# The first two modulation sections by column blocks, and the first three output chunks k-pair by k-pair

## The reference, cut to what matters

```python
c_act = silu(c)                                   # (1, 2048)
for layer in range(2):
    mod = c_act @ ada_w[layer] + ada_b[layer]     # (2048 x 12288) weights
    shift_t, scale_t, gate_t, shift_m, scale_m, gate_m = split(mod, 6)
    h = rms_norm(x, norm_g[layer, 0]) * (1 + scale_t) + shift_t
    y = mixer(h, ...)                             # layer 0: qkv = h @ w_qkv
    x = x + gate_t * y
    h = rms_norm(x, norm_g[layer, 1]) * (1 + scale_m) + shift_m
    x = x + gate_m * square(relu(h @ w1)) @ w2
```

## Time and profile before

| | us |
|---|---|
| median of three runs (2586.28 to 2590.52) | 2586.66 |
| the profiled execution: its own time | 2587.83 |
| its span, first to last instruction | 2586.0 |
| TensorE busy | 2403.0 (93%) |
| VectorE busy | 1848.6 (71%) |
| ScalarE busy | 1185.4 (46%) |
| bytes moved | 665.23 MB, 257 GB/s over the span |

### The profile page before, as it was taken

How to read it: one execution, slowest core, us unless ns; L and a number is a source line. 1 busy time by engine, 2 the same in 40 slices (tenths; PEclk the granted TensorE clock), 3 DMA queues, 4 the chain that set the end, 5 groups by cost and what they waited for, 6 DMA issues and landing times.

```text
span 2586.0 us, 27843 instructions
## 1 busy us (share of the span) xinstructions
PE 2403.0 (93%) x10901; PEld 1970.1 (76%) x10901; DVE 1848.6 (71%) x2145; ACT 1185.4 (46%) x1931; POOL 72.9 (3%) x128
## 2 busy tenths in 40 slices
PE   0299999997999999999998989999899999999999
PEld 0288888876787888888887877777687888888887
DVE  7778786877788677677776767877796555555554
ACT  1256556564543443443445664554543443443442
POOL 1100000000100000000001010000100000000000
PEclk9599999999999999999999999999999999999999
DMA  8688696866788777777785867856696555555554
GB/s 358 270 296 306 220 342 233 328 252 236 292 302 308 261 282 275 276 289 267 280 301 207 316 230 282 312 210 254 263 368 211 189 187 187 187 186 188 187 187 163
DMA packets 150466, 665.23 MB, mean 257 GB/s; under 512 B 16864, under 2 KB 17344, under 8 KB 120896
## 3 DMA queue, kind: packets, MB, share of 16 engines
q1 hardware_dynamic: 150336, 663.46, 70.3%
HBM read 661.30 MB, written 2.10 MB: 257 GB/s over the span
## 4 chain that ended last, share of the span: by engine, by line
PE 75%; DVE 12%; ACT 5%; DMA 4%; issue 4%; POOL 0%; SPq 0%; DVEq 0%; ACTq 0%
PE main L359 24%; PE main L361 24%; PE main L360 24%; DVE acc L916 5%; DVE w_lo L899 3%; DMA w_raw<-w 2%; PE tr L372 2%; ACT w_hi L644 1%; DMA ada_raw<-ada 1%; ACT st_a L684 1%; PE tr L414 1%; DMA qT<-ada 1%; ACT sm L717 1%; PE tr L435 0%; ACT st_b L670 0%
## 5 line engine op out<-in xcount | busy, mean ns | idle before, releaser
L644 ACT ACTIVATE w_hi<-w_raw 128x1024 fp32r<-128x1024 f32 x800 | 844.1, 1060 | 1105.0 <-DMA w_raw<-w 1104.6
L899 DVE TENSOR_TENSOR w_lo<-w_raw,w_hi 128x1024 fp32r<-128x1024 f32 x800 | 971.6, 1222 | 438.4 <-ACT w_hi L644 434.9
L359 PE MATMUL main<-w_hi,hT_hi 128*128 128x512 f32 x2176 | 869.4, 400 | 7.0 <-DVE w_lo L899 2.9
L361 PE MATMUL main<-w_hi,hT_lo 128*128 128x512 f32 x2176 | 851.5, 391 | 0.0
L360 PE MATMUL main<-w_lo,hT_hi 128*128 128x512 f32 x2176 | 850.8, 391 | 0.0
L916 DVE SCALAR_TENSOR_TENSOR acc<-ada_raw,c_act,acc 128x2048 f32<-128x2048 f32 x194 | 455.7, 2349 | 50.2 <-DMA ada_raw<-ada 47.8
L359 PEld LDWEIGHTS main<-w_hi,hT_hi 128*128 128x128 f32 x2176 | 411.6, 189 | 93.4 <-DVE w_lo L899 5.2
L361 PEld LDWEIGHTS main<-w_hi,hT_lo 128*128 128x128 f32 x2176 | 410.5, 189 | 86.9
L360 PEld LDWEIGHTS main<-w_lo,hT_hi 128*128 128x128 f32 x2176 | 411.3, 189 | 83.4 <-issue 1.2
L359 PE MATMUL main<-w_hi,mid_hi 128*128 128x512 f32 x1024 | 406.1, 397 | 0.0
L361 PE MATMUL main<-w_hi,mid_lo 128*128 128x512 f32 x1024 | 404.0, 395 | 0.0
(11 more groups left out here) (155 smaller groups left out, 1166.7 us busy)
## 6 DMA issues: line engine op xcount, KB each, us to landing
w_raw<-w SPq DMA_DIRECT2D x800, 512.0 KB, 3.4
ada_raw<-ada SPq DMA_DIRECT2D x208, 1024.0 KB, 6.5
qT<-ada SPq DMA_DIRECT2D x16, 1024.0 KB, 7.2
gate<-bias_rows SPq DMA_DIRECT2D x4, 1024.0 KB, 6.5
xs<-x SPq DMA_DIRECT2D x1, 2048.0 KB, 9.2
out<-xs SPq DMA_DIRECT2D x4, 512.0 KB, 5.3
st_a<-lamb SPq DMA_DIRECT2D x1, 256.0 KB, 4.7
gain_rot_sb<-gain_rot SPq DMA_DIRECT2D x1, 160.0 KB, 2.9
```

The source lines that it names most:

```text
L359: pe.matmul(acc_ps[:, :], hi[:, kt, tc], w_hi[:, s, wc], start=(kt == 0), stop=False)
L361: last = pe.matmul(acc_ps[:, :], lo[:, kt, tc], w_hi[:, s, wc], start=False, stop=(kt == PK * pairs - 1))
L644: act.activation(w_hi[:, s, :], w_raw[:, s, :], ACT.Copy).then_inc(hi_done, 1)
L899: dve.tensor_tensor(w_lo[:, s, :], w_raw[:, s, :], w_hi[:, s, :].bitcast(F32), ALU.subtract).then_inc(lo_done, 1)
```

## The change

- The host lays out the first two sections of `ada` by column blocks. Round j (0 to 7) has four pieces of 1 MB, a = 0 to 3. Piece a holds four k-tiles, and of each the 256 shift and 256 scale columns that belong to pair j of k-tiles of `h`.
- Of a piece's four k-tiles VectorE adds three (two of the last piece) into 512 columns of `acc`, each step waiting for the one before; TensorE does the rest as f32 products with one moving column, four for each k-tile (`first_columns`), and sums `acc` over partitions with a column of ones (`first_total`). Both accumulate in one bank, `tr[1]`. VectorE then makes the 2 + 2 columns of factor and shift for pair j (`first_modulation`).
- The first three chunks (q, k, v of quad 0) arrive interleaved: for each pair of k-tiles a piece of q, of k and of v, between pieces a=1 and a=2 of the round. TensorE multiplies pair j-1 in round j (`first_piece`) into six banks: `main[1]`, `main[0]`, and `sc` with `ov`.
- x is loaded second; the gains come after the 32 pieces; ScalarE squares x before the angles. The zero attention step is dropped.
- After the first stage q and k of quad 0 are read out of `main`, and v out of `sc`, `ov`, during chunk 3. The 48 later `ada` pieces of this stage go to the 15 chunks left: 2, 3, 4, 4 in group 0; 3, 3, 4, 3, 3, 3 in group 1; 3, 3, 4, 3, 3 in group 2. Two sections are then in work at once; the second is summed in `gate`.

```diff
@@ host layout
+    first = [np.concatenate([w[:, cols(j, PK * P)] for w in ada[0:2]], axis=1) for j in range(PIECES)]
+    ada[0:2] = [w.reshape(FIRST_PIECES, KT // FIRST_PIECES, P, NC).transpose(0, 2, 1, 3).reshape(-1, D) for w in first]
+    stream[0:3] = [np.stack([w.reshape(PIECES, P, PK * NC) for w in stream[0:3]], axis=1).reshape(-1, PK * NC)]
@@ constants
-ADA_QKV = after((0, 5, 7), (0, 5, 7), (0, 2, 4, 6), (0, 5, 7), (0, 5, 7))
+FIRST_PIECES = 4
+PE_TILES = (1, 1, 1, 2)
+ADA_QKV = [((g, c), j) for g, c, js in (
+    (0, 2, (0, 7)), (0, 3, (0, 5, 7)), (0, 4, (0, 2, 5, 7)), (0, 5, (0, 1, 2, 7)), (1, 0, (0, 5, 7)),
+    (1, 1, (0, 5, 7)), (1, 2, (0, 2, 4, 6)), (1, 3, (0, 5, 7)), (1, 4, (0, 5, 7)), (1, 5, (0, 2, 7)),
+    (2, 0, (0, 5, 7)), (2, 1, (0, 5, 7)), (2, 2, (0, 2, 4, 6)), (2, 3, (0, 5, 7)), (2, 4, (0, 5, 7))) for j in js]
@@ sync
+            def first_ada(i):
+                s = i % len(ada_start)
+                if i >= len(ada_start):
+                    sp.wait_ge(ada_used, ADA_SLOTS + i + 1 - len(ada_start))
+                    sp.wait_ge(ada_mm, i + 1 - len(ada_start))
+                sp.dma_start(ada_start[s], av[i]).then_inc(ada_start_in[s], 16)
+            for j in range(PIECES):
+                for a in range(FIRST_PIECES):
+                    if a == 2:
+                        for _ in range(3):
+                            weight_piece()
+                    first_ada(FIRST_PIECES * j + a)
...
+            sp.wait_ge(ada_mm, 2 * KT)
@@ tensor
+            def first_columns(j, a):
+                i = FIRST_PIECES * j + a
+                fills, s = divmod(i, len(ada_start))
+                pe.wait_ge(ada_start_in[s], 16 * (fills + 1))
+                last = None
+                for k in range(FIRST_PIECES - PE_TILES[a], FIRST_PIECES):
+                    kt = FIRST_PIECES * a + k
+                    for c in range(4):
+                        last = pe.matmul(tr[1][:, 4 * j + c:4 * j + c + 1],
+                                         ada_start[s][:, k * NC + c * P:k * NC + (c + 1) * P],
+                                         c_act[:, kt:kt + 1], start=(a == 0 and last is None), stop=False)
+                last.then_inc(ada_mm, 1)
+            def first_total(j):
+                pe.wait_ge(ada_used, ADA_SLOTS + FIRST_PIECES * (j + 1))
+                for c in range(4):
+                    at = (j % 2) * NC + c * P
+                    last = pe.matmul(tr[1][:, 4 * j + c:4 * j + c + 1], acc[:, at:at + P], ones[:, 0:1],
+                                     start=False, stop=(c == 3))
+                last.then_inc(col_full, 1)
+            def first_piece(j, part):
...
+                if part == 0:
+                    pe.wait_ge(hT_split, n["split"].up())
+                pe.wait_ge(lo_done, n["w"].n)
+                banks = (main[1], main[0], (sc, ov))[part]
+                for kt in range(PK * j, PK * (j + 1)):
...
+            for j in range(PIECES):
+                if j:
+                    pe.wait_ge(mod_done, j)
+                first_columns(j, 0)
+                first_columns(j, 1)
+                if j:
+                    first_piece(j - 1, 0)
+                first_transposes(j)
+                if j:
+                    first_piece(j - 1, 1)
+                    first_piece(j - 1, 2)
+                first_columns(j, 2)
+                first_columns(j, 3)
+                first_total(j)
+            for part in range(3):
+                first_piece(PIECES - 1, part)
@@ scalar
+            for j in range(PIECES):
+                for _ in range(3):
+                    split()
+                high(j, (S_SCALE_T0, S_SHIFT_T0), True)()
+            act.wait_ge(gain_in, 16 * 3)
...
+                    chunk(PIECES, {3: [qk_stats(1, 5), qk_scale(1)], 5: [move_tile0(q4, g), qk_stats(0, 6)],
+                                   6: [qk_scale(0)], 7: [first_values], 8: [move_tile0(k4, GROUPS + g)]})
@@ vector
+            for j in range(PIECES):
+                first_ada(j, 0)
+                if j == 0:
+                    sum_x()
+                else:
+                    pair(j - 1, True)()
+                first_ada(j, 1)
+                if j == 0:
+                    x_recip()
+                for _ in range(3):
+                    split()
+                first_ada(j, 2)
...
+                first_ada(j, 3)
+                first_modulation(j)
```

More of the change, by code:

```diff
@@ L297, in _ @@
+            sp.dma_start(subg[:, :], subg_in.partition_broadcast(P)).then_inc(gain_in, 16)
+            sp.wait_ge(ada_mm, 2 * KT)
+            for g in range(GROUPS):
+                for c in range(0 if g else 2, 6 if g < GROUPS - 1 else 5):
+                    if (g, c) == (GROUPS - 1, 2):
+                        sp.wait_ge(scale_added, 1)
+                        bias(0, 0)
+                    chunk((g, c), ada=ADA_QKV)
             for ch in range(4):
@@ new lines, in first_piece @@
+            def first_piece(j, part):
+                if j == 0 and part < 2:
+                    claim_main(1 - part)
+                if j == 0 and part == 2:
+                    pe.wait_ge(x_sq, 4)
+                if part == 0:
+                    pe.wait_ge(hT_split, n["split"].up())
+                n["w"].up()
+                s = (n["w"].n - 1) % SLOTS
+                pe.wait_ge(lo_done, n["w"].n)
+                banks = (main[1], main[0], (sc, ov))[part]
+                for kt in range(PK * j, PK * (j + 1)):
+                    wc = cols(kt % PK, NC)
+                    for t in range(T):
+                        tc = cols(t, P)
+                        pe.matmul(banks[t][:, :], hT_hi[:, kt, tc], w_hi[:, s, wc], start=(kt == 0), stop=False)
+                        pe.matmul(banks[t][:, :], hT_hi[:, kt, tc], w_lo[:, s, wc], start=False, stop=False)
+                        last = pe.matmul(banks[t][:, :], hT_lo[:, kt, tc], w_hi[:, s, wc], start=False,
+                                         stop=(kt == KT - 1))
+                last.then_inc(mm_done, 1)
@@ L788, in _ @@
             act.activation(c_act[:, :], vec[:, V_C, :], ACT.Exp, scale=-1.0).then_inc(c_exp, 1)
+            act.wait_ge(x_in_done, 16)
+            for c in range(4):
+                squares(c)
+            root()
             act.wait_ge(lam_dot, 1)
@@ L915, in accumulate, with first_ada @@
                     dve.wait_ge(ada_used, a - 1 + ADA_SLOTS)
-                    ins = dve.scalar_tensor_tensor(out=acc[:, :], in0=piece, scalar=c_act[:, kt:kt + 1],
-                                                   in1=acc[:, :], op0=ALU.mult, op1=ALU.add)
+                    ins = dve.scalar_tensor_tensor(out=total[:, :], in0=piece, scalar=c_act[:, kt:kt + 1],
+                                                   in1=total[:, :], op0=ALU.mult, op1=ALU.add)
                 ins.then_inc(ada_used, 1)
-            def chunk(ch, pieces, side=None, ada=(), kt0=0):
+            def first_ada(j, a):
+                i = FIRST_PIECES * j + a
+                fills, s = divmod(i, len(ada_start))
+                dve.wait_ge(ada_start_in[s], 16 * (fills + 1))
+                total = acc[:, cols(j % 2, NC)]
+                tiles = FIRST_PIECES - PE_TILES[a]
+                for k in range(tiles):
+                    piece, c = ada_start[s][:, cols(k, NC)], c_act[:, FIRST_PIECES * a + k:FIRST_PIECES * a + k + 1]
+                    if a == 0 and k == 0:
+                        ins = dve.tensor_scalar(total, piece, c, None, ALU.mult)
+                    else:
+                        if k == 0:
+                            dve.wait_ge(ada_used, ADA_SLOTS + i)
+                        ins = dve.scalar_tensor_tensor(out=total, in0=piece, scalar=c, in1=total,
+                                                       op0=ALU.mult, op1=ALU.add)
+                    if k < tiles - 1:
+                        chained(ins)
+                ins.then_inc(ada_used, 1)
@@ new lines, in first_modulation @@
+            def first_modulation(j):
+                dve.wait_ge(col_full, n["col"].up())
+                at = slice(PK * j, PK * (j + 1))
+                both = modc[:, S_SHIFT_T0:S_SCALE_T0 + 1, at]
+                chained(dve.tensor_tensor(both, both, tr[1][:, 4 * j:4 * j + 4].rearrange("p (s k) -> p s k", s=2),
+                                          ALU.add))
+                scale = modc[:, S_SCALE_T0, at]
+                dve.scalar_tensor_tensor(out=scale, in0=scale, scalar=1.0, in1=vec[:, V_G, at],
+                                         op0=ALU.add, op1=ALU.mult).then_inc(mod_done, 1)
@@ L922, in chunk @@
+            def chunk(ch, pieces, side=None, ada=(), kt0=0, totals=(acc,)):
                 for j in range(pieces + 1):
@@ L1083, in low, with pair, step @@
                                   ALU.subtract).then_inc(done, 1)
+            def pair(j, first=False):
+                def step():
+                    dve.wait_ge(hi_part, n["hi"].up())
```

(5 more changed lines are left out.)

180 lines of the change are left out of this document (86 added, 94 removed).

## The result

The changed kernel takes 2593.13 us (median of ten executions, 2586.65 to 2595.8), the kernel before 2586.6 (ten, on the same chip). The ratio is 1.0023, with a 95% interval of 1.0014 to 1.0033: slower, by little more than the 0.2% that I called the bound. Forecast was 2564.2, range 2547 to 2581, and slower had a chance of 0.1.

What follows compares the result with a forecast made beforehand. TensorE, busy 2403 of 2586.0 us, was taken as the bound wherever it runs, leaving some 118 us before its first product to win. Gain 29.2 less 6.7 given back, net 22.5, gave 2564.2 us; range 2547 to 2581.

Steps and rivals of the forecast that it cites:

- given back: From chunk 3 on: transposes 1.7, q's read-out 1, ScalarE in chunk 3 1, later `ada` pieces 3; 6.7 us.
- the start: Before the first round's modulation: engines, not bytes, decide; first `mod_done` at 30 us, bounds 26 and 34.
- the dense chunks: The 15 later chunks carrying 48 `ada` pieces, those with four lacking slack: 3 us lost, bounds 0 and 12.
- The circle: Chain through all engines from one modulation to the next, setting the round: 15.9 us, 17.4 with the clock's fall.
- the eight column products of a=0 and a=1 lie in this time: Round's start, ahead of q: TensorE's products fit the 2.9 us until `hT_split`, if each costs below 0.36 us.
- the mark: End of the third chunk, where the kernels are compared: 193.3 us before, forecast 164.1.
- the rival that was built on it: Rounds of the first stage: the clock holds, round 15.9 us, total 2552 us; chance 0.2.
- 1 with hand-over: Chunk 3's first products wait for q's read-out, ready at 164.6 against 164.1: 1 us lost.
- 9 into 13.4. It fits: 260 to 290 us: five added pieces less column sums, 9 us, fit VectorE's 13.4 us free.
- The rival of dense chunks: Groups 0 and 1: `w_lo` late, ten chunks lose 1 us each, 4 in chunk 3; 2572 to 2578; chance 0.15.
- The rival that decided: Rounds: column products at 0.45 us each add 4.3 us a round, 30 us, total 2594; chance 0.1.
- the rival of late transfers: Rounds: last weights or `ada` come late through one queue; rounds 20 us, mark 182, total 2584; chance 0.05.

Runs made afterwards that it cites:

- v late: Changed kernel with v's piece multiplied after the column products of a=2 and a=3 instead of ahead of them: 2594.82 us, 1.0037 of the kernel before.
- two repairs: Changed kernel with two quarters of the column sums moved to step 1, rotation ahead of a `w_lo`, and square-root table loaded early: 2574.49 us, 0.9959 of before.
- (1, 0, 1, 1): Changed kernel with two repairs, and TensorE's k-tiles for pieces a=0 to 3 set so from (1, 1, 1, 2): 2565.55 us, 0.9925 of before.
- (0, 0, 1, 2): Changed kernel with two repairs, and TensorE's k-tiles set so, VectorE adding all of a=0 and a=1: 2579.51 us, 0.9973 of before.

## Why the prediction was wrong

The stage was forecast to gain 29.2 us and gained 18.9; 6.7 were to be given back and it was 20.8 in the profiled execution. The 24.4 us between forecast and measurement are 3.2 in the start, 6.4 in the rounds, 0.7 at the end of the stage, 4.4 in the chunk of the hand-over (8.1 against 1.7 + 1 + 1) and 9.7 in the dense chunks (12.7 against 3). The median is 28.9 above the forecast: the tail was 3.0 shorter in the profile, and the profiled executions lie 1.2 above the median before and 6.5 below it after.

**The start.** Forecast: `mod_done` at 30. The second small step of the modulation ends at 33.2. ScalarE loads four function tables of 1.28 us each, three of them between the squares and the sines; the kernel before has three in its start, since it took the root after the sines. I had added the squares' time and the root's table, but not that the exponential then needs its table a second time (L881, 1.28 us, at 17.61). The first split starts at 21.60 against my 20 to 21, VectorE ends a=3 at 30.85 against 28.6, and the total is cold, 1.86 us, against 1.2 with drain.

**The circle.** Its order held, and four of its six terms are within 0.15 us. A round of 17.87 us, from 106.37 to 124.24:

| term | forecast | measured |
|---|---|---|
| modulation, until q starts | 0.45 + 2.9 | 3.57 |
| q's piece with the clock's loss | 2.73 + 1.5 | 4.70 |
| transposes | 0.5 | 0.35 |
| k and v | 5.46 | 5.58 |
| twelve column products | 2.7 | 2.60 |
| total | 1.2 | 1.07 |
| sum | 17.4 | 17.87 |

In the rounds of 18.8 the first is 3.84 and the second 5.27. The step that failed is "the eight column products of a=0 and a=1 lie in this time, if they cost below 0.36 us each". The price, 0.225, was right warm, and at the price that they had here the condition was not met. I had the clock fall in every round and charged its loss to the large products alone. These eight come behind the fall, cost 0.41 to 0.45 us each, and put q off by 0.5 to 0.8 against the 3.04 us at which the block of h lets it start; taking four of them away gave this back. Since I had taken 3.35 for that wait, the term is only 0.2 to 0.5 over the forecast. The larger part of what a round lacks is the next term: the clock's loss in q's piece, taken as 1.5, is 1.97 and 2.54. The rise comes 3.8 us into q's piece in this round and over 5 in the longer ones, not at 3.3: the row that I took the earlier trace rows is a single rise. Seven rounds: 128.2 us against 121.8, 6.4 us. The end of the stage took 13.0 against 12.3. 3.2, 6.4 and 0.7 are the 10.3 us that the mark lacks.

**The clock.** That it falls was right, as was 0.7 to 0.9 in the rounds (0.74 to 0.83 from 51 us on; ahead of that the windows show 1.00 although column products take 0.22 a record, so there I go by the durations). In a window of 20 us (60 to 80) TensorE is busy for 19.55 and the clock is 0.83. The Trainium skill's advice for bursts ("TensorE: Matmul & The Clock Gate", section "HAM oscillation"), to leave no long idle gap between them, doesn't suffice here: the trace disagrees with the reading for idle time alone, and the rival that was built on it is refuted. The kernel with v late shows it best: a fall between two large products with no pause ahead of it.

**The hand-over.** "1 with hand-over" was 6: 4.35 us of idle time, and 1.5 of cold products. I had followed what `read_out` needs on ScalarE and never asked what stands ahead of `rope` in VectorE's queue. I had also left out the table load between sine and root, 1.28 us. The `qk_transposes` are 1.7 as forecast; the two together give 7.6 of the 8.1 that are lost by the read-out of chunk 3. (The sum of the forecast has a slip of no weight: 158.6 + 2.4 + 0.3 + 2.2 + 0.9 is 164.4, not 164.6.)

**The dense chunks.** "9 into 13.4. It fits" is the step that cost most: 3 forecast, 12.7 measured (8.1 + 5.6 + 1.4 less 2.4 won), just outside the bounds of 0 to 12. I had looked at whether VectorE's free time would hold the added pieces, and it does: with the same pieces and the sums earlier, 10 of the 12.7 us are gone. What counted was the order: a step that TensorE waits for stands in VectorE's queue behind pieces that no one waits for. The forecast took the column sums out of the stretch at 260 to 290 ("less its column sums") and had no term for the place that they went to. The rival of dense chunks had the place right but the mechanism wrong (`w_lo` late by 1 us in each of ten chunks): one wait of 4.29 us and one of 1.86, each with cold products behind it (clock 0.89 from 330 to 345, 0.86 from 468 to 480), not many small ones.

**The rival that decided.** Slower was forecast to come from a column product of 0.45 us. They reach that price, but only the eight ahead of q, and that is worth some 4 us (0.6 in each of seven rounds) by which q is late. The slower kernel is thus not this rival come true. (For the rival of late transfers the text has 2584; its own mark of 182 gives 2582.) No single rival of mine gave the outcome; it is 10 us less at the stage and 14 us more given back, misses of one sign. The range took in the cases of the gain, but for what is given back only one value.

**What the change is worth.** With two repairs that change nothing else than the order of a few instructions and one early table load, the kernel is 0.41% faster than before, and with the tiles at (1, 0, 1, 1) 0.75% (0.62 to 0.88): 2565.55, close to the 2564.2 that was forecast for the kernel as it stood, which is chance. The kernel before did not run with its sums moved; its two waits for them are 2.7 us, at clock 1.00, so this repair alone could hardly give it the 12.6 us that lie between the two, but that is argued and not shown.

**What stays open.** The tail of the kernel, which the change doesn't touch, varies by up to 8 us between the profiled executions of all kernels (1989.0 to 1997.1 us from the last reciprocal of the value step on). One difference lies where the clock is 0.93 in one and 0.96 in another (from 1360 to 1560); I didn't look into what starts it. The wait for the masks of 1.5 or 3 us is likewise not traced to its cause. From 180 to 590 us TensorE's waits for the copies of `pT` on VectorE grew from 1.5 us in the kernel before to 4.5 in the changed one, and no run takes them away. And no run separates why q's piece stays cold longer in one round than in the next.

## What to carry to other kernels

When work is moved onto an engine with time to spare, its share of busy time tells only whether it fits; list what is queued there ahead of each instruction that another engine waits for, and put these ahead of the work that no one waits for. Pauses of 1.86 to 4.35 us on TensorE cost here the pause and another 1.5 to 3 us of cold products behind it, and a forecast should have both. And if the clock is taken to fall in a stretch, everything that follows until it rises is priced at the low clock, small instructions too.

## What the runs showed of the hardware

- An f32 product with one moving column is two records of 0.114 us each at clock 1.00 and 0.206 to 0.223 at the low one. Warm, that is the price of an f32 product of 128 columns: going from 128 moving columns to one saves nothing.
- The clock fell with TensorE at work: after 2.74 us of column products and about 1.5 us of large ones (v late). Where column products stood one for one among large ones, a window of 4 us of them had clock 1.00.
- The rise came 3.3 us (kernel before) to 6 us (v late, from 112.8 to 118.9) after large products had begun. In one kernel, (0, 0, 1, 2), 3.8 and over 5 us took turns from round to round, so that rounds came as 18.2 and 19.2 us.
- Waits of 1.34 us (kernel before) and 1.54 us left the clock at 1.00. One of 1.86 us, at the scale sums, was followed by products of 0.63 us, and so was one of 2.96 us at the place of the 1.54, with 0.89 over the 30 us around it.
- A load of a function table took 1.28 us on ScalarE, and the activation behind it started at its end (171.77 to 173.06).
